# Low parts of the expert weights on VectorE alone, and an expert's places made earlier, in a single-core transformer kernel

## The reference

```
logits = h @ w_router + b_router                 # 256 x 8
top_val, top_idx = top_k(logits, 2); gates = softmax(top_val)
for each expert e of 8:                          # on the tokens that chose e
    y = (silu(x_e @ w_gate[e]) * (x_e @ w_up[e])) @ w_down[e]    # 1024 -> 1408 -> 1024
    out[tokens of e] += gate * y
```

## Time and profile before

| | |
|---|---|
| time, median of 3 runs | 2301.41 us (2300.39 to 2301.81) |
| the profiled execution | 2300.23 us, of which its span is 2298.3 us |
| PE busy | 2086.5 us, 91% of the span |
| DVE busy | 1354.7 us, 59% |
| ACT busy | 1049.1 us, 46% |
| POOL busy | 437.8 us, 19% |
| experts, from the first GpSimd low part to the last scatter | about 1790 to 2276 us |

### The profile page before, as it was taken

The page is one execution under the profiler, slowest core; times in us unless marked ns, Lnnn a source line. Parts: engine busy times, 40 slices in busy tenths (PEclk is TensorE's granted clock), DMA queues, the critical chain, the costliest instruction groups (busy, mean ns, idle before and its releaser), DMA issues.

```text
span 2298.3 us, 33465 instructions
## 1 busy us (share of the span) xinstructions
PE 2086.5 (91%) x13808; PEld 1784.4 (78%) x13808; DVE 1354.7 (59%) x1999; ACT 1049.1 (46%) x1681; POOL 437.8 (19%) x335
## 2 busy tenths in 40 slices
PE   5998989899999899999988979999778999989996
PEld 3775777787788765899988879999768777777775
DVE  1349448765644447577556554444574777776784
ACT  2347433232333325466455234444353665656663
POOL 0301031100100320222013212101000333333341
PEclk8999999898999899999998989999887999999998
DMA  6330334444422111245533014554422677767783
GB/s 279 120 129 6 142 129 154 146 176 165 150 107 85 68 63 50 94 177 183 203 129 129 3 64 165 185 185 147 187 107 96 236 295 274 274 259 277 276 319 115
DMA packets 52672, 364.86 MB, mean 159 GB/s; under 512 B 5921, under 2 KB 8225, under 8 KB 8865
## 3 DMA queue, kind: packets, MB, share of 16 engines
q1 hardware_dynamic: 49488, 357.06, 42.1%
q10 hardware_dynamic: 3024, 5.57, 0.7%
HBM read 361.56 MB, written 1.05 MB: 158 GB/s over the span
## 4 chain that ended last, share of the span: by engine, by line
PE 73%; DVE 9%; ACT 6%; POOL 6%; issue 4%; DMA 2%; ACTq 0%; DVEq 0%; POOLq 0%; SPq 0%
PE ps L77 19%; PE ps L78 18%; PE ps L79 18%; PE ps L74 17%; POOL WLO L91 4%; ACT WHI L85 4%; PE ps L82 2%; DVE WLO L91 2%; DVE R L88 2%; ACT R L85 2%; DVE SM L105 1%; DVE R L91 1%; DMA ring<-W 1%; POOL R L91 1%; POOL h L95 1%
## 5 line engine op out<-in xcount | busy, mean ns | idle before, releaser
L91 DVE TENSOR_TENSOR WLO<-ring,WHI 128x1024 fp32r<-128x1024 f32 x492 | 668.5, 1381 | 285.9 <-ACT WHI L85 284.9
L85 ACT ACTIVATE WHI<-ring 128x1024 fp32r<-128x1024 f32 x557 | 568.6, 1052 | 153.8 <-PE ps L79 132.4
L77 PE MATMUL ps<-HHI,WHI 128*128 128x256 f32 (+1 forms) x1680 | 550.1, 327 | 34.3 <-DVE WLO L91 13.3
L78 PE MATMUL ps<-HLO,WHI 128*128 128x256 f32 (+1 forms) x1744 | 561.8, 322 | 0.0
L79 PE MATMUL ps<-HHI,WLO 128*128 128x256 f32 (+1 forms) x1680 | 542.6, 323 | 0.0
L77 PEld LDWEIGHTS ps<-HHI,WHI 128*128 128x128 f32 x1680 | 331.6, 197 | 72.1 <-issue 42.0
L78 PEld LDWEIGHTS ps<-HLO,WHI 128*128 128x128 f32 x1744 | 344.0, 197 | 20.8
L79 PEld LDWEIGHTS ps<-HHI,WLO 128*128 128x128 f32 x1680 | 330.9, 197 | 22.1
L74 PE MATMUL ps<-R 64*64 64x64 f32 (+12 forms) x2832 | 251.9, 293 | 23.1 <-DVE R L96 16.9
L91 POOL TENSOR_TENSOR WLO<-ring,WHI 128x1024 fp32r<-128x1024 f32 x65 | 175.9, 2706 | 361.9 <-ACT WHI L85 361.9
L74 PEld LDWEIGHTS ps<-R 64*64 64x64 f32 (+5 forms) x2832 | 189.9, 158 | 65.4 <-issue 32.9
(11 more groups left out here) (165 smaller groups left out, 2937.2 us busy)
## 6 DMA issues: line engine op xcount, KB each, us to landing
ring<-W SPq DMA_DIRECT2D x340, 1024.0 KB, 4.9
x<-xt ACTq DMA_DIRECT2D x1, 2048.0 KB, 12.8
CR<-const_nsa ACTq DMA_DIRECT2D x1, 560.0 KB, 5.1
out<-x SPq DMA_DIRECT2D x1, 512.0 KB, 3.0
out<-x ACTq DMA_DIRECT2D x1, 512.0 KB, 3.0
CR<-const_rw ACTq DMA_DIRECT2D x1, 448.0 KB, 3.5
CR<-const_gqa ACTq DMA_DIRECT2D x1, 320.0 KB, 3.9
CR<-const_mla ACTq DMA_DIRECT2D x1, 320.0 KB, 2.8
```

What stands on the lines that cost most here:

```text
L77: self.e.matmul(out, l[0], r[0], start=start, stop=False)
L78: self.e.matmul(out, l[0], r[1], start=False, stop=False)
L85: return self.e.activation(out, in_, func, **kw)
L91: return self.e.tensor_tensor(out, in0, in1, op)
```

## The change

Every low part is now made by VectorE, and GpSimd has no work in the experts. The places of expert e+1 are made by VectorE within `up(e)`, in its second block (nb = 1) after the turn, instead of in `gather(e+1)`; those of expert 0 stay where they were.

```diff
@@ class Feed, unit
-        self.units.append([c, UNIT * odd, self.share and len(self.own) % 4 == 3, 0])
+        self.units.append([c, UNIT * odd, False, 0])
@@ lo_units
-    def lo_units(e, units, pool=False):
+    def lo_units(e, units):
         for u in units:
-            c, col, pooled, _ = F.units[u]
-            if pooled != pool:
-                continue
+            c, col, _, _ = F.units[u]
...
             e.tt(WLO[:, o:o + UNIT], src, WHI[:, o:o + UNIT], ALU.subtract).then_inc(
-                *did("w_lo_pool" if pool else "w_lo", ("lo", u)))
+                *did("w_lo", ("lo", u)))
@@ experts_dve
-        def gather(e):
+        def places(e):
             i = e % 2
             if e >= 2:
                 v.wait_ge(*at("gathered", r, e - 2))
...
             t.then_inc(*did("places", ("places", r, e)))
+
+        def gather(e):
+            i = e % 2
+            if e == 0:
+                places(0)
             for half in range(2):
                 v.wait_ge(*at("xhi", r, e, half))
...
         def up(e):
             for nb, (_, wd) in enumerate(BLOCKS):
                 lo_units(v, st.ahead[up_group(e, nb, 0)])
                 turn_after(e, nb, turn)
+                if nb == 1 and e < 7:
+                    places(e + 1)
                 lo_units(v, st.ahead[up_group(e, nb, 1)])
@@ experts_pool and its two calls in gpsimd
-    def experts_pool(g, r):
-        st = L["moe", r]
-        lo_units(g, st.first, True)
-        for more in st.ahead:
-            lo_units(g, more, True)
...
-        experts_pool(g, 0)
-        second_pass(g, experts_pool)
```

## The result

The changed kernel takes 2262.57 us (median of 4 runs, 2261.55 to 2266.03) against 2301.61 us before in the same session: a ratio of 0.9827 with a 95% interval of 0.9815 to 0.9839, so 39 us or 1.7% faster. The forecast was 2274 us in a range of 2259 to 2288.

What follows compares the result with a forecast made beforehand. TensorE was taken as the bound, its waits as the gain: 2300.2 - 27.2 (GpSimd's low parts) - 13.9 (places) + 13.9 (added waits) = 2273.0, so 2274 us as median; range 2259 to 2288.

Steps and rivals of the forecast that it cites:

- The bound: In the experts TensorE sets the pace, its records covering 57.3 of 62.1 us; only its gaps can be gained.
- VectorE's slow low parts go with GpSimd: In the experts, VectorE's low parts fall from a mean of 1.584 to 1.22 us; its load grows only 16 us.
- New waits of TensorE: TensorE waits for VectorE's low parts behind gathers, turns and ends of `down`: 19.4 us in sum, bounds 9.7 to 38.8.
- The term that was mis-sized: In the experts, TensorE's waits for VectorE's low parts: 19.4 us in place of 5.5, so 13.9 us more.
- The places: Moving them from between scatter and gather into the up-projection frees 13.9 us of TensorE's idle time, over seven waits.
- The new waits hardly appear: Rival: TensorE's waits for VectorE's low parts come at half price, 9.7 us; 2256 to 2266 us; chance 0.17.
- my own case: The forecast's central band for the whole kernel, 2266 to 2282 us around 2274; chance 0.58.
- The ring becomes the limit: Rival: DMA chunks limit the experts, costing 2 us more for each; 2284 to 2292 us; chance 0.13.
- What is freed is used up: Rival: TensorE's waits in the experts, 41.1 us, are only renamed; about 2301 us; chance 0.06.
- Slower, VectorE the bound: Rival: VectorE's low parts stay at 1.584 us, so an expert takes 64.5 us; 2320 us; chance 0.06.
- the point from which it decides: In the experts, the time per low part, 1.51 us, from which VectorE sets the pace.

Runs made afterwards that it cites:

- reading beside: Changed kernel plus two GpSimd 128 x 512 subtractions of a constant tile for each fourth unit, nothing waiting for them: 2300.79 us.
- writing beside: Changed kernel plus two GpSimd 128 x 512 memsets for each fourth unit, nothing waiting for them: 2261.94 us.
- the places later: Changed kernel with the next expert's places made in the third block, before its turn, instead of in the second after it: 2257.24 us.

## Why the prediction was right, and where its size was off

**The bound.** "TensorE is the bound and its gaps are what can be gained": held. The granted clock stayed at 1.00 between the gathers.

**VectorE's slow low parts go with GpSimd.** Held and shown by the pair of GpSimd runs: reading beside brings the mean back to 1568 ns, writing beside leaves it at 1219. The trace of the kernel before shows it part by part: 54 of VectorE's low parts took over 1.3 us, and each of them ended 1.08 to 1.09 us after the GpSimd part that was running when it began. The prediction's "315 us after, against 298.5 before" sets a product of number and mean beside a busy time, in which overlapping records count once. Like with like it is 306 to 317 us by the products (193 x 1.584, 260 x 1.220), or 298.5 to 301.4 by the busy time: still less growth than the 16 us that were named.

**New waits of TensorE.** The list was right in its places and nearly in its prices. It named 31, and the trace has 24 waits for VectorE and 7 that it calls issue, but that both are 31 is luck: behind the ends of `down` there are six, not eight, and two (0.26 and 0.42 us) stand at places that were not on the list. A weight load's wait less 0.16 is what it costs: behind a turn with places 1.23 - 0.16 = 1.07 us where 1.24 was worked out, behind other turns 0.45 - 0.16 = 0.29 against 0.43, behind a gather 0.61 - 0.16 = 0.45 against 0.49, behind a `down` 0.66 - 0.16 = 0.50 against the 0.43 that was chosen. In sum 21.6 - 31 x 0.16 = 16.6 us, forecast 19.4.

**The term that was mis-sized** is the one set against this: "In sum 19.4 us, in place of today's 5.5 us: 13.9 us more". Of the waits before I had counted only those put down to GpSimd and VectorE. A third row of the same view was left out:

```profile
PEld ps L77 <- issue: 8.3, 14, 1.9
```

It is 8.3 us in 14 waits; less 0.16 for each that is 6.1 us. Today's waits were 5.5 + 6.1 = 11.6, and the new ones add 16.6 - 11.6 = 5.0 us, not 13.9. The longest of the 14, in the kernel before:

```profile
2008.57 2.37 POOL L91 TENSOR_TENSOR WLO<-ring,WHI 128x1024 fp32r<-128x1024 f32 x1 [4.74 <-ACT WHI L85]
...
2011.06 0.19 PEld L77 LDWEIGHTS ps<-WHI,XSHI 128*128 128x128 f32 x1 [1.85 <-issue]
2011.09 0.47 PE L77 MATMUL ps<-WHI,XSHI 128*128 128x512 f32 x1 [1.46 <-POOL WLO L91]
```

The weight load starts 0.12 us after the end of a GpSimd part, and its matmul is put down to that part. Eight of the 14 start 0.11 to 0.12 us behind the end of a GpSimd part like this one, 5.0 us in all, or 3.7 after the 0.16: they are waits for GpSimd under another name. So the 5.0 us can be split: GpSimd's parts cost 27.2 + 3.7 = 30.9 us, and the waits of the kind that stays went from 5.5 + 2.4 = 7.9 to 16.6, by 8.7. Of the 13.9 - 5.0 = 8.9 us by which the term was off, 6.1 are this row and 2.8 the lower prices.

**The places.** 13.9 us went as worked out. Not counted was that a gather that starts out of a wait costs more than the wait: its 32 matmuls take 3.85 us in the chain before, 3.58 in the chain after, which is 7 x 0.27 = 1.9 us. From the first start to the last it is 3.56 us and 3.46; the other 0.17 us are overlap with the matmul in front, which a gather out of a wait does without.

**The balance.** The experts: 27.2 + 13.9 + 1.9 - 5.0 = 38.0 us, against 40.7 measured; 2.7 us are not traced. Ahead of the experts the profile after is 3.1 us slower, within what the profiles of the same instructions differ by. 40.7 - 3.1 = 37.6 is the difference of the spans.

**The rivals.** *The new waits hardly appear* gave 2256 to 2266 us and the time lies in it, yet not by its mechanism: the waits did appear, at 16.6 us where it had 9.7. That my range of 2259 to 2288 held although my own case, 2266 to 2282, missed by 3 us is because the range took in most of this rival. *The ring becomes the limit* fell: ScalarE waited 3.2 us for DMA. *What is freed is used up* fell. *Slower, VectorE the bound* fell, but the run with GpSimd's reads shows its mechanism at work: at a mean of 1.568 us a part VectorE is the bound. I had put the point from which it decides at 1.51 us, which fits. By the same working, 52.5 + 33 x 0.348 = 64.0 us for an expert, the price was too high: 62.6 were measured.

## What to carry to other kernels

Before giving a share of work to a slower engine, read the duration of the same instruction on the engine that it relieves, its median beside its mean: a mean of 1584 ns over a median of 1219 said that the help cost VectorE 70 us for the 79 (65 x 1.22) it saved. Work that a busy engine has to do in order belongs where it waits anyway (the places in front of the third turn), and it is worth trying one more unit in stock: in the experts it brought 22 us in the kernel before and 10.9 us in the one with the places later, with the same four buffers. When new waits are set against old ones, count every row of the waits that names the waiting instruction, "issue" too.

## What the runs showed of the hardware

While a GpSimd instruction that reads SBUF runs, a VectorE instruction with two SBUF inputs stands still: all 54 slow low parts of the kernel before ended 1.08 to 1.09 us after GpSimd's. It works the other way too: GpSimd's part took 2.37 to 2.41 us where it began with no low part of VectorE under way, and up to 3.32 us where one was. Instructions with one input from PSUM (`HDLO`, the hidden values, the additions to x) are spared: 17 of them overlapped a GpSimd part, and none took over 0.69 us. The price was more than I had expected: 130 subtractions of 128 x 512 for which nothing waited cost 38 us of 2262. 130 memsets cost nothing. The Trainium skill has both in "SBUF — State Buffer", "Who interferes with whom", where a GpSimd instruction that only writes is said not to contend with such a VectorE instruction; both runs agree. A memset is not free beside every instruction, though: of the 28 that make the places three overlapped memsets, and two of these took 0.63 and 0.44 us, where 0.34 is the median.
